# Gates laid out in DRAM by load instead of by store, in a decoder layer with product-key experts

## What is computed

```
s = einsum('thpd,hpkd->thpk', q, keys)          # 8 heads, 2 x 128 keys per token
sv, si = top_k(s, 16)                           # 16 of 128 on each side
cv, ci = top_k(sv[:, :, 0, :, None] + sv[:, :, 1, None, :], 16)
eidx = i1 * 128 + i2                            # 128 experts of 16384 per token
gate = softmax(cv)
h = gelu(einsum('tkd,td->tk', u_tab[eidx], x))
out = einsum('tk,tkd->td', gate * h, v_tab[eidx])
```

## Time and profile before

| | us |
|---|---|
| median of 3 runs | 2267.47 (2265.25 to 2269.86) |
| profiled execution, its time | 2268.81 |
| profiled execution, its span | 2267.0 |

### The profile page before, as it was taken

How to read it: one execution, slowest core, us unless ns; L and a number is a source line. 1 busy time by engine, 2 the same in 40 slices (tenths; PEclk the granted TensorE clock), 3 DMA queues, 4 the chain that set the end, 5 groups by cost and what they waited for, 6 DMA issues and landing times. The chain is left out here.

```text
span 2267.0 us, 29766 instructions
## 1 busy us (share of the span) xinstructions
PE 1967.8 (87%) x11493; PEld 1795.5 (79%) x11493; DVE 1519.0 (67%) x2533; ACT 885.7 (39%) x1752; POOL 798.1 (35%) x440
## 2 busy tenths in 40 slices
PE   4999479848888997899999988888838999999998
PEld 4999479728787687899999988888737887877777
DVE  3676444270333213198999989999647887988886
ACT  2455112121433013233443458888414343434333
POOL 0333114002541022167878764444531222222220
PEclk8999679869999999999999999999978999999999
DMA  4221100022452502157998978888989999999994
GB/s 127 66 75 41 45 1 1 5 83 75 130 205 62 180 29 75 72 167 290 352 355 319 361 275 310 307 317 306 379 334 374 402 402 371 386 402 402 396 401 171
DMA packets 211500, 513.01 MB, mean 226 GB/s; under 512 B 13216, under 2 KB 143008, under 8 KB 174496
## 3 DMA queue, kind: packets, MB, share of 16 engines
q1 hardware_dynamic: 172768, 259.43, 33.8%
q0 software_dynamic: 27648, 201.34, 22.6%
q10 hardware_dynamic: 10944, 50.34, 5.6%
HBM read 451.26 MB, written 59.80 MB: 225 GB/s over the span
## 5 line engine op out<-in xcount | busy, mean ns | idle before, releaser
L1556 POOL TENSOR_TENSOR ex_ulo<-ex_u,ex_uhi 128x1024 fp32r<-128x1024 f32 x128 | 332.3, 2600 | 271.3 <-ACT ex_uhi L1582 270.6
L1668 PE MATMUL ps<-xhi,ex_uhi 128*128 128x384 f32 x1024 | 356.5, 348 | 36.7 <-ACT ex_h L1611 23.5
L1668 PE MATMUL ps<-xlo,ex_uhi 128*128 128x384 f32 x1024 | 347.0, 339 | 0.0
L1668 PE MATMUL ps<-xhi,ex_ulo 128*128 128x384 f32 x1024 | 346.8, 339 | 0.0
L1295 POOL DMA_INDIRECT ga_ring<-in_uv,ga_idx x138 | 176.0, 1275 | 315.2 <-DVE po_acc_s L1321 171.9
L1968 PE MATMUL ps<-po_vhi,po_whi 128*128 128x512 f32 x768 | 240.1, 394 | 48.6 <-DVE po_wlo L2002 47.4
L1935 ACT CAST po_vhi<-po_v 128x1024 fp32r<-128x1024 f32 x128 | 133.7, 1046 | 320.5 <-DMA po_v<-in_peer_v 295.4
L1968 PE MATMUL ps<-po_vlo,po_whi 128*128 128x512 f32 x768 | 237.9, 391 | 0.0
L1968 PE MATMUL ps<-po_vhi,po_wlo 128*128 128x512 f32 x768 | 237.8, 391 | 0.0
L1668 PEld LDWEIGHTS ps<-xhi,ex_uhi 128*128 128x128 f32 x1024 | 196.3, 192 | 40.4 <-issue 26.1
L1968 PEld LDWEIGHTS ps<-po_vhi,po_whi 128*128 128x128 f32 x768 | 143.9, 189 | 84.3 <-issue 53.7
(11 more groups left out here) (392 smaller groups left out, 4271.1 us busy)
## 6 DMA issues: line engine op xcount, KB each, us to landing
ex_u<-in_uT SPq DMA_DIRECT2D x128, 512.0 KB
po_v<-in_peer_v SPq DMA_DIRECT2D x64, 1024.0 KB, 11.9
acts<-ex_h ACTq DMA_DIRECT2D x64, 384.0 KB
gates<-scores ACTq DMA_DIRECT2D x12, 2048.0 KB, 11.4
po_w<-acts SPq DMA_DIRECT2D x32, 768.0 KB, 12.5
po_g<-gates SPq DMA_DIRECT2D x32, 768.0 KB, 15.8
in_w_raw<-in_w_in SPq DMA_DIRECT2D x24, 512.0 KB
at_cache<-in_cacheT SPq DMA_DIRECT2D x6, 1024.0 KB, 6.6
```

The lines of the kernel that those rows point to most:

```text
L1556: pool.tensor_tensor(ulo[:, j % 3], u[:, j % 3], uhi[:, j % 3].bitcast(F32), ALU.subtract).then_inc(low, 1)
L1668: mm = pe.matmul(ps[:, j % 2, 0:ND], w[:, j % 3, k, :], x[:, k, :], start=(k == 0 and n == 0), stop=(k == KT - 1 and n == 2))
```

## The change

The DRAM tensor `gates` is laid out as group of four keys, partition, group of 32 tokens, key in the group, token. What the output block loads for one partition is then one piece of 6 KB instead of 12 pieces of 512 bytes; what the experts block stores for one partition goes to 32 places of 512 bytes instead of one of 16 KB. The number of DMAs, the bytes and the layouts in SBUF are as before.

```diff
+        g_store = io["gates"].rearrange("q p g e t -> g p q e t")
...
-                        act.dma_start(io["gates"][g], spread[g % 2]).then_inc(spread_stored[g % 2], 16)
+                        act.dma_start(g_store[g], spread[g % 2].rearrange("p (q e) t -> p q e t", e=4)).then_inc(spread_stored[g % 2], 16)
...
-        g_dram = io["gates"].rearrange("k p e t -> p k e t")
...
-                sp.dma_start(g_sb[:, q % 2], g_dram[:, :, 4 * q:4 * q + 4, :]).then_inc(gg_loaded[q % 2], 16)
+                sp.dma_start(g_sb[:, q % 2], io["gates"][q]).then_inc(gg_loaded[q % 2], 16)
...
-    io["gates"] = nc.dram_tensor("gates", [ND // 32, P, P, 32], F32, kind="Internal").ap()
+    io["gates"] = nc.dram_tensor("gates", [NKEY // 4, P, ND // 32, 4, 32], F32, kind="Internal").ap()
```

## The result

| | before | changed |
|---|---|---|
| median of 7 runs each, us | 2265.25 (2251.39 to 2269.86) | 2287.31 (2270.20 to 2305.31) |
| ratio changed/before | | 1.0091, 95% interval 1.0048 to 1.0133 |
| profiled execution, us (span) | 2268.81 (2267.0) | 2291.02 (2289.2) |
| start of the output block (SP's first load) | 1686.39 | 1727.93 |
| PE's first matmul there | 1708.33 | 1744.69 |

The change made the kernel slower by 0.9%: 22.1 us between the medians and 22.2 us between the two profiled executions. The prediction was 2276, with 2252 to 2292 as its range. One of the seven runs of the changed kernel, the one of 2305.31 us, was in a slower state of the chip and is left out of the ratio; the mean of the six others is 20.5 us above that of the kernel before.

A forecast was written before the change was run, and what follows sets the result against it. The output block's loads were taken to set the pace, with PE nearly the bound. Loads -12 us, that block's start -0.7 and ACT's holds +21.2 gave +8.5 us, thus a median of 2276 us, range 2252 to 2292.

The forecast's parts named there:

- Rival A: Experts block: the queue doesn't hold ACT behind gate stores, so only the gains remain: 2254.8 us, 2252 to 2262; chance 0.34.
- Rival C: Experts block: each gate store holds itself until its packets fit, some 6 us in 11 places: 2321 us; chance 0.08.
- Rival D: Output block: the changed loads give nothing; 2267 us without the hold, 2288 with it; chance 0.10.
- cover: Experts block: 1.6 us of each hold hidden, from the end of PE's quads to DVE's pair that needs them.
- The loads: Output block: gate loads in 6 KB pieces bring transfers level with PE's pace: -12 us.
- the bound of 14.1: Output block: the most faster loads can give after its start, 12.4 us of PE idle plus 1.7 of clock.
- Start of the output block: PE's wait before its first matmul there shortens by what the first gate load saves: -0.7 us.
- The hold: Experts block: ACT held 6.9 us at an acts store behind four gate stores, 5.3 us lost each, +21.2 us.
- 2292 case: Experts block: all 257 packets must be through beside gathers, hold 10 us, three middle places add 1.5 each: 2292 us.
- The release at 100 per engine left: ACT's queue: an issue waits while more than about 100 packets per engine of its queue are unfinished.
- A middle place: Experts block: one of three gate stores with the acts store 6.7 us behind; expected not held, 0 us.
- B: Experts block: ACT is held behind gate stores at four places: 2263 to 2292 us; chance 0.48.

The follow-up runs named there:

- e3: The changed kernel with its 12 gate stores issued by SP instead of ACT: 2255.51 us, ratio 0.9947 to the kernel before.
- e4: The changed kernel with four gate stores issued right behind the acts store that had followed them, not ahead of it: 2250.31 us, ratio 0.9940 to the kernel before.
- e1: The kernel before with only the gate loads changed, to 6 KB rows (gates permuted): 2241.48 us, ratio 0.9889.
- e7: The kernel before with POOL's first three gathers of the output block held until the first gate load has landed: 2268.38 us, one execution.
- e5: The changed kernel with gate stores in 2048 pieces of 1 KB, 129 packets per engine (gates permuted): 2277.32 us, one execution.
- e9: e5 with each gate store cut into two DMAs, 81 packets per engine first and 49 two quads later: 2259.85 us, one execution.
- e11: e5 with each gate store cut into two DMAs, 113 packets per engine first and 17 two quads later: 2258.72 us, one execution.
- e2: The kernel before with only the gate stores changed, loads still in 512-byte pieces but of the new memory (gates permuted): 2309.02 us, ratio 1.0200.
- e8: The changed kernel with each gate store issued in four DMAs, one behind each of the next four evictions: 2265.94 us, ratio 0.9999 to the kernel before.

## Why the prediction was right in its sign and short in its size

**Right.** The packets of both queues, to the last one. Rival A is out: ACT's queue is held (four acts stores of over 6 us), and without that e3 and e4 are faster than the kernel before. Rival C is out: L1638 itself takes 0.38 us. Rival D is out: e1 gains 1.1%. The DMA time of the small stores is hidden to within some 5 us (e3). The place, the four gate stores with an acts store 1.98 us behind, is the one where it happens, and the condition that decides (a hold above 4.8 us on the mean) was met by 9.6 us. That the point lies there is luck: it was worked out with a gain of 12.7 us and a cover of 1.6; with the measured gain of 19.3 and no cover it is 19.3/4 = 4.8 us as well, above the usual 0.33.

**The loads: -12 predicted, -14.1 measured.** From PE's first matmul to the end of the output block's matmuls of L1968 it went from 548.7 to 534.6 us. The mechanism was right: 512-byte pieces kept the transfers behind PE, and with large ones PE is the bound. The same number as the bound of 14.1 is partly luck, since it is not made of the same parts. The bound was 12.4 us of idle time and 1.7 of clock. PE's waits in the block fell by 9.1 us, from 12.4 in 15 times to one of 3.3 at 1766 (with a granted clock of 0.59 in the 4 us from 1766). The other 5.0 are less busy time; that there are fewer restarts and less slow clock fits it, but they weren't told apart. PE's pace is 1998 matmuls in 452.89 us, 0.2267 us each, so 16.3 us for four keys. The prediction had 16.2, from a count of matmuls in a window that takes in those cut by its ends, and 16.3 for the transfers. The DMA share is still 1.01 at 415 GB/s, so the transfers are close behind PE: in stretches of 520 us ACT's waits for v fell from 264.0 to 141.1 us, and its waits for PE to free a buffer rose from 21.6 to 152.4.

**Start of the output block: -0.7 predicted, -5.2 measured** (21.94 to 16.76 us from SP's first load to PE's first matmul). I gave g(0) the 0.74 us of the full rate. Its last small packets passed beside the gathers at some 6 in a microsecond, for 8 us; e7, which takes the gathers away and leaves the small pieces, gains 6.4 us there. That is the mechanism of this term, and it is the one that is missing from the next.

**The hold: 6.9 us predicted, 12.77, 10.30, 6.56 and 8.85 measured.** This is the term that was mis-sized. The four parts of it:
- The start of the drain (3.8 us after the issue) holds: the store at 1369.01 moves 14 packets in the microsecond from 1372 and 266 in the next, the one at 1522.77 moves 94 in that from 1526.
- The rate of 31 per engine and us, taken from one window of the kernel before, holds only while the store has the engines nearly to itself. At the third place it does; at the first it doesn't. The packets of the changed kernel from 1528 to 1529 us, then from 1380 to 1381:

```profile
q10 hardware_dynamic: 680, 0.35, 114.8%
```

```profile
q0 software_dynamic: 42, 0.34, 88.9%
q10 hardware_dynamic: 43, 0.02, 7.3%
```

  680 packets in a microsecond alone, 16/680 = 23.5 ns each; 43 beside the gathers' 8 KB packets. In the four microseconds from 1378 on, with u loads and then gathers beside them, 360 packets moved where 2700 would have. The prediction knew that gathers fill the engines when it set the 3.8 us and, in its 2292 case, that they take part of the drain; it did not carry that to the price of a small packet. The rows for it were in the kernel before: 6 small packets in a microsecond at 1695, 480 in the earlier trace rows.
- The release at 100 per engine left is a guess from the earlier trace rows and is wrong as a rule (e5, e9 to e11). At the undisturbed third place about 1216 packets, 76 per engine on the mean, were left when the hold ended. That its 6.56 us are near the 6.9 is luck: the drain was faster than taken (680 packets per microsecond, not 493) and the release later (76 left, not 100). At the first, the second and the fourth place 27, 16 and 42 were left. A mean over engines can hide one that is late, as the tail of g(0) above suggests, but the trace's queue rows don't part the engines: argued, not shown.
- The cover of 1.6 us was nil. I read it off one chain, from the quads' end to DVE's pair. Right behind each hold DVE waits a second time for PE's quads (8.1 us in 5 times, above): the slack that the pair had lent for the first eviction was gone for the second. The loss is 37.4 us against holds of 37.2.

Taken together, 4 x 5.3 = 21.2 became 37.4.

**Smaller terms.** A middle place is held once, for 2.59 us at 1432.79, and costs 0.5; I had counted 0 and kept 1.5 each for the upper end. From the twelfth gate store to the output block it is 2.6 us longer; I had counted nothing. The acts store there is held 12.77 us, but whether the hold costs this isn't shown: e2, held for 11.78 us, needs 0.6 us more than the kernel before, e4, held for 11.68, 4.4 more. The first gate store is 1.1 us later, most of it (0.8) before the experts block. The parts divide one and the same difference of times, 37.4 + 0.5 + 2.6 + 1.1 = 41.5 but for rounding, and 41.5 - 5.2 - 14.1 = 22.2 us. They confirm no cause; the experiments do that.

The estimate for the hold of 10 us, with gathers in the drain, was my 2292 case; the mean of the four is 9.6. The errors in the loss (+16 in the holds, +4 beside them) and in the gain (-4.5 at the start, -2.1 in the loads) carry +8.5 to +22.2: right in sign, and within the range of B by 5 us. The upper end of that range is itself short by its own terms: 2267.5 + 38 - 12.7 is 2292.8.

**Not settled.** The count that the queue goes by and when it lets go; whether stores in 512-byte pieces that hold nobody still cost a few us (e4 against e1); and where the 5.0 us of busy time in the output block went.

## What to carry to other kernels

When a DMA is cut into smaller pieces, count its descriptors per engine and look at what is issued next on the same queue: the DMA itself may cost next to nothing, and the short one behind it stalls the engine that issues both. Put the long DMA behind the urgent one, or on a queue whose engine has time; here that turned a loss of 0.9% into a gain of 0.6%, about half of what the loads alone gave. Where an early part of the program varies from run to run, compare the lengths of blocks, not the moments at which they start. And price small packets by the traffic of that moment: their rate alone and beside large packets of other queues differ by more than ten.

## What the runs showed of the hardware

- Writes in pieces of 512 bytes move at 348 GB/s alone (680 per us). I had taken 28.5 ns per packet from loads; it is 23.5.
- Beside gathers of 8 KB packets the same writes move at 43 per us, reads of 512 bytes at 49 per us: about one small packet for each large one of the other queue (43 to 42, 49 to 46). It holds for three queues as well: from 1655 to 1656 us of the changed kernel the queues q0, q1 and q10 have 34, 34 and 36 packets and 0.25, 0.14 and 0.02 MB. So a queue of small packets gets a share by their size, not a half. The Trainium skill (DMA: Bandwidth & Descriptors, Queues, rings and completion order) says that each engine goes round its queues by packets, and counts some 9 to 17 descriptors to one. The rows agree that the queues take turns. The turns they show are of one piece each, since the profile's packets are single pieces here (4096 + 16 per gate store). The prediction didn't weigh this, and it is what made the hold long at the first place.
- ACT is held at a DMA behind an unfinished one of 81 to 257 packets per engine, for 2.3 to 12.8 us, not behind a single one of 65; behind several of 65 it was held for up to 6.17 us (e8). The Trainium skill (Perfetto Trace Analysis, DMA Instruction - HWDGE) has the time shown for a DMA run until all its descriptors are made, and lets the DMA engines begin earlier when more are made than the buffer takes. By that one would look for the long time at the DMA that fills the buffer. Here that one, with 257 packets per engine, keeps 0.38 us, and the DMA behind it, with 9, shows up to 12.77.
- With gaps of up to 13 us on PE the granted clock of the stage is 0.93 on the mean from 1345 to 1600 us, where e4 without them has 1.00.
